# Hybrid retention / attention / mixture-of-experts layer: the low halves of four weight chunks per expert block split between VectorE and GpSimd

## The chip, the cores and the metric

One Trainium2 chip, one NeuronCore. The metric is the device time of one execution in microseconds (us). The engines are called as in the profile: PE (TensorE matmul), PEld (its weight loads), DVE (VectorE), ACT (ScalarE), POOL (GpSimd) and SP (SyncE, which only issues transfers here). A letter q behind an engine means its sequencer.

## The reference, cut to what matters

The layer takes 512 latent tokens and 256 context tokens of width 1024, runs retention and differential attention side by side, merges them, and ends in a mixture of 32 experts with the 4 best experts for each token. Only this last stage is changed:

```
logits = xt @ router_w + router_b;  gate = softmax(top_4(logits))
# token/expert pairs sorted by expert, each expert's group padded to blocks of 128 rows
hh  = xblk @ w1[e] + b1[e]                  # 128x1024 @ 1024x2048
glu = min(hh[:, :1024], 7);  lin = clip(hh[:, 1024:], -7, 7)
act = glu * sigmoid(1.702 * glu) * (lin + 1)
y   = act @ w2[e] + b2[e]                   # 128x1024 @ 1024x1024
out = x_new + g_f * segment_sum(y * gate)
```

All of it is float32. With these inputs there are 33 blocks of 128 rows (32 experts, one of which needs two blocks).

## The kernel before, in words

A float32 product is made of three products of split numbers. ACT rounds a weight chunk to fp32r (the high part, `e_whi`, written by `hi_e`, L1040 and L1041). DVE subtracts it from the chunk as loaded, which gives the low part (`e_wlo`, written by `lo_e`, L1589). PE then multiplies high by high, high by low and low by high (`mm`, L1662).

A weight chunk is 128 partitions x 2048 columns, 1 MB. Each block uses 12 of them: chunks 0 to 7 are w1 (`up`), chunks 8 to 11 are w2 (`down`). Raw chunks lie in 6 slots (`e_raw`), high and low parts in 4 slots each. The loads are issued on SP in the order of the chunks, and a load waits until the low part of the chunk six before it is made (`e_lo`), since that frees its slot. The timeline calls the slots of the parts `whi`, `hhi`, `wlo` and `hlo`; raw chunks are `raw` or `ar`.

Around block i the engines work in this order, all of it written out by hand, each engine in order:

- PE: `up(i)`, which goes chunk by chunk and within a chunk over four groups of 512 columns; then the 8 transposes of the next x (`turn_x`, L2017), `down` of the block before, the 8 transposes of this block's activation (`turn_act`, L2025), and `up(i + 1)`.
- DVE: low part of block i - 1's activation (`act_low`, L1616), low parts of chunks 4 to 10, then `activate`, which begins when `up(i)` has ended: L1600 twice, the low part of chunk 11, L1603, L1606 and L1610 twice each; then the low part of the next x (`x_low`, L1581, twice) and the low parts of chunks 0 to 3 of the next block.
- ACT: the high parts in the same order, the tanh (L1054), the high part of the next x (L1049), then the high parts of chunks 0 to 3 of the next block, and the scaled copy of the output row block, `give_y` (L1067).
- POOL: the bias selector (`next_sel`, L770), the gather of the rows of the block after next (`next_gather`, L777 and L749), the scattered add of a finished block into the result in memory (`scatter`, L786), a wait for that add to land, and the copy of the next list of row numbers (`cur`, L798).

`turn_act` waits for `x_low` (`xt_lo`), since both use the same PSUM banks, and `up(i + 1)` starts when the low part of its chunk 0 is there:

```
    for kk in range(KC):
        pe.wait_ge(e_lo, chunk(i, kk) + 1)
        for b in range(4):
```

Operands of the instructions spoken of below: L1606 and L1610 (`scalar_tensor_tensor`) and L1589 (`tensor_tensor`) read two SBUF tensors; L1600 and L1603 read PSUM; L1581 and L1616 read one PSUM and one SBUF tensor. In the attention stage, POOL squares a 128x512 tile (L722, `tensor_tensor`, two SBUF inputs) and raises 128x8 numbers to a power (L700), while DVE scales and rotates (L1332 to L1351, two SBUF inputs each).

Of the kernel before, what the change touches and what calls it, by code (L numbers as in the profile page):

```python
# [21 lines left out]
F32 = mybir.dt.float32  # L22
# [4 lines left out]
ALU = mybir.AluOpType  # L27
# [3 lines left out]
P = 128  # L31
D = 1024
KC = D // P
L = 512
# [5 lines left out]
COL = 512  # L40
# [3 lines left out]
ERAW = 6  # L44
# [29 lines left out]
OUT0 = GB0 + 4  # L74
MOE0, MOE_N = OUT0 + 4, 12
FIRST = 8


C_ID = 0
# [62 lines left out]
def chunk(i, j):  # L142

    return j if isinstance(i, int) and i == 0 else i * MOE_N - (MOE_N - FIRST) + j

# [11 lines left out]
def raw_slot(i, j):  # L157

    return j % ERAW if isinstance(i, int) and i == 0 else (j - (MOE_N - FIRST)) % ERAW

# [15 lines left out]
def build(nc, a, scratch):  # L176
    mod_d, h2_d, list_d, acc_d, accr_d = scratch
    ctx = ExitStack()
    with ctx:
# [3 lines left out]
        def sem(name):  # L183
            return ctx.enter_context(nc.semaphore(name))
# [63 lines left out]
        e_loaded = [sem(f"e_loaded{k}") for k in range(ERAW)]  # L248
        e_hi = sem("e_hi")
        e_lo = sem("e_lo")  # L250
        e_used = sem("e_used")

        dve_pre = sem("dve_pre")
# [252 lines left out]
        def _(sp):  # L506
# [85 lines left out]
            def load_w1(e, i, j):  # L592

                if isinstance(i, int) and i == 0 and j < NRAW:
                    sp.wait_ge(hi_made, OUT0 - RET0 + j + 1)
                    sp.wait_ge(lo_made, OUT0 - RET0 + j + 1)
                elif not isinstance(i, int) or j >= ERAW:
                    sp.wait_ge(e_lo, chunk(i, j) - ERAW + 1)
                sp.dma_start(e_raw[raw_slot(i, j)], a["exp_w1"][one(e), j * P:(j + 1) * P, :].rearrange(
                    "o p n -> p (o n)")).then_inc(e_loaded[raw_slot(i, j)], 16)  # L600

            def load_w2(e, i, j, k):

                sp.wait_ge(e_lo, chunk(i, j) - ERAW + 1)
                sp.dma_start(e_raw[raw_slot(i, j)].rearrange("p (a n) -> p a n", a=2),
                             a["exp_w2"][one(e), k * 2 * P:(k + 1) * 2 * P, :].rearrange(
                                 "o (a p) n -> p (o a) n", p=P)).then_inc(e_loaded[raw_slot(i, j)], 16)
# [36 lines left out]


            sp.wait_ge(gathered, n_items * 16 + 32)
            sp.wait_ge(y_added, n_items * 16)
            for t in range(LT):
                sp.dma_start(F(A_XG if t == 0 else A_Y if t == 1 else A_GS if t == 2 else A_HT, D),
                             acc_d[t * P:(t + 1) * P, :]).then_inc(acc_back[t], 16)  # L650
# [7 lines left out]
        def _(pool):  # L658
# [32 lines left out]
            def hold():  # L691

                pool.sem_inc(pool_tick, 1)
# [10 lines left out]
            rstd(ss[:, 0:TT], TT, D, st).then_inc(x_rstd, 1)  # L704
            pool.wait_ge(mod_used, 2 * MOD_A + 2)
            pool.wait_ge(pool_pre, ZEROED)
            pool.dma_start(h2_d[L:L + P, :], F(A_ACC, D)).then_inc(s_init, 16)
            pool.dma_start(acc_d[L:L + P, :], F(A_ACC, D)).then_inc(s_init, 16)
            with pool.Fori(0, RET_HEADS) as h:
                pool.wait_ge(o_sq, at(h, LT, LT))  # L710
                rstd(ss[:, 0:LT], LT, DV, Steps(pool, pool_r, h)).then_inc(o_rstd, 1)
# [45 lines left out]
                pool.wait_ge(h2_stored[k], 16 * LT // 2)  # L757
            gather()

            pool.tensor_copy(cur[:, :], listsb[:, 0, :]).then_inc(cur_ready, 1)  # L760
            pool.wait_ge(xt_turned, 2)
            pool.wait_ge(gathered, 16)
            pool.tensor_copy(nxt[:, :], listsb[:, 1, :]).then_inc(pool_m, 1)
# [9 lines left out]
            def next_gather(i, code2):  # L773
# [6 lines left out]
                hold()  # L780
                gather()

            def scatter(i):
                pool.wait_ge(y_out, i * 2 + 2)
                hold()
                pool.indirect_dma_start(acc_d, bass.IndirectOffsetOnAxis(ap=cur[:, 0:1], axis=0),  # L786
                                        F(A_Y, D), None, compute_op=ALU.add).then_inc(y_added, 16)
                pool.wait_ge(y_added, i * 16)
                hold()

            def item(i):
                code = pool.value_load(items_i[0:1, bass.ds(i, 1)], min_val=0, max_val=4 * N_EXPERTS - 1)
                e1 = pool.value_load(items_i[0:1, bass.ds(i + ITEMS + 1, 1)], min_val=0, max_val=N_EXPERTS - 1)
                code2 = pool.value_load(items_i[0:1, bass.ds(i + 2, 1)], min_val=0, max_val=4 * N_EXPERTS - 1)
                next_sel(i, e1)
                next_gather(i, code2)
                scatter(i)
                pool.tensor_copy(cur[:, :], listsb[:, bass.ds(code, 1), :].rearrange(  # L798
                    "p o w -> p (o w)")).then_inc(cur_ready, 1)

            next_sel(0, 1)
            next_gather(0, 2)
            pool.wait_ge(acc_init, 16 * LT)
            with pool.Fori(1, N_EXPERTS) as i:
                item(i)
            with pool.Fori(N_EXPERTS, MAX_BLOCKS) as i:
                with pool.If(i < n_items):
                    item(i)
            scatter(n_items)
            pool.wait_ge(gathered, n_items * 16 + 32)  # L810
            hold()
# [306 lines left out]
        def _(dve):  # L1118
# [105 lines left out]
            lo(RET0, RET_N, 0, 0)  # L1224
            mod_row(11)
            acc = F(A_ACC, KC, L)
            dve.wait_ge(s_init, 16 * (4 + 2))
            dve.wait_ge(h_lo, 2 * KC)
            RS = 7
            with dve.Fori(0, RET_HEADS) as h:  # L1230
# [353 lines left out]
            def lo_e(i, j):  # L1584

                s = raw_slot(i, j)
                dve.wait_ge(e_hi, chunk(i, j) + 1)
                dve.wait_ge(e_loaded[s], rounds(i, j) * 16 + 16)
                V.tensor_tensor(e_wlo[j % ESPL], e_raw[s], e_whi[j % ESPL].bitcast(F32),  # L1589
                                ALU.subtract).then_inc(e_lo, 1)  # L1590

            MS = 4
# [67 lines left out]
        def _(pe):  # L1660
# [368 lines left out]
            def up(i):  # L2029
                pe.wait_ge(sel_ready, i + 1)  # L2030
                for kk in range(KC):
                    pe.wait_ge(e_lo, chunk(i, kk) + 1)
                    for b in range(4):
                        o = ps[:, 2 + b, :]
                        cols = slice(b * COL, (b + 1) * COL)
                        wh, wl = e_whi[kk % ESPL][:, cols], e_wlo[kk % ESPL][:, cols]
                        if kk == 0:
                            last = mm(o, sel[0:96, :], bias[0:96, cols], True, False)
                            if b == 3:
                                last.then_inc(sel_used, 1)  # L2040
                        mm(o, xthi[:, kk, :], wh, False, False)
                        mm(o, xthi[:, kk, :], wl, False, False)
                        last = mm(o, xtlo[:, kk, :], wh, False, kk == KC - 1)
                    last.then_inc(e_used, 1)

            def down(i, at_i, j0):
                pe.wait_ge(act_lo, i * 2 + 2)
                pe.wait_ge(y_out, i * 2 + 2)
                for k in range(MOE_N - FIRST):
                    j = j0 + k  # L2050
                    pe.wait_ge(e_lo, chunk(at_i, j) + 1)
                    for q in range(2):
                        kk = 2 * k + q
                        for c in range(2):
                            o = ps[:, 6 + c, :]
                            cols = slice(q * D + c * COL, q * D + (c + 1) * COL)
                            wh, wl = e_whi[j % ESPL][:, cols], e_wlo[j % ESPL][:, cols]
                            mm(o, acthi[:, kk, :], wh, kk == 0, False)
                            mm(o, acthi[:, kk, :], wl, False, False)
                            last = mm(o, actlo[:, kk, :], wh, False, kk == KC - 1)  # L2060
                    last.then_inc(e_used, 1)
# [112 lines left out]
```

## Time and profile before

| | |
|---|---|
| time, median of 3 | 2650.99 us (2650.47 to 2651.24) |
| the profiled execution | 2651.42 us, span 2649.8 us |
| mean granted clock of TensorE | 0.961 |
| busy: PE, PEld | 2394.2 us (90%), 1842.1 us (70%) |
| busy: DVE, ACT, POOL | 1709.2 us (65%), 1235.8 us (47%), 511.3 us (19%) |
| memory read | 535.65 MB |

The expert stage fills the second half of the span, from about 1380 us to 2630 us. How to read it: the shares are means over all stages; PE is close to full in the expert stage, and the rows below show where it is not. A timeline row gives start, duration, engine, line, what is written and read, the count of merged instructions, and in brackets the idle time before it and what ended it.

### The profile page before, as it was taken

What the parts mean: (1) busy time and instruction counts of PE and PEld (TensorE: products, weight loads), DVE (VectorE), ACT (ScalarE), POOL (GpSimd) and SP (SyncE); (2) the same over time, 40 slices, a digit from 0 to 9 for tenths busy, and PEclk for the clock granted to TensorE, in tenths of its full rate; (3) what the DMA queues carried; (4) which work ended last, traced back from release to release, by engine and by line L of the source; (5) the groups of instructions that cost most, each with busy time, mean ns of one, the idle gap of its engine ahead of it and who ended that gap; (6) DMA issues with size and microseconds to landing.
All of it is one profiled execution on the core that took longest, in us unless ns stands there. A gap on an engine that the chain in (4) does not pass through costs nothing.

```text
span 2649.8 us, 31314 instructions
## 1 busy us (share of the span) xinstructions
PE 2394.2 (90%) x10564; PEld 1842.1 (70%) x10564; DVE 1709.2 (65%) x1667; ACT 1235.8 (47%) x1215; POOL 511.3 (19%) x313
## 2 busy tenths in 40 slices
PE   5999999999998779769878999999999999999994
PEld 1385858677686667657757777777777777777773
DVE  1433324233246635553748999999999999999994
ACT  1221122121122522352236767777677767777672
POOL 2000000000023003100031233333233233322331
PEclk9999999999999889899959999999999999999997
DMA  8811211112131001003347999999999999999994
GB/s 259 301 65 41 70 47 63 63 47 79 43 116 54 11 33 64 32 1 135 135 148 301 375 362 358 370 367 374 362 358 375 370 368 361 364 371 375 361 359 164
DMA packets 145976, 563.29 MB, mean 213 GB/s; under 512 B 17698, under 2 KB 25890, under 8 KB 111842
## 3 DMA queue, kind: packets, MB, share of 16 engines
q1 hardware_dynamic: 127536, 518.05, 51.4%
q0 software_dynamic: 11280, 38.21, 5.4%
q10 hardware_dynamic: 7112, 6.37, 0.8%
q8 instruction: 33, 0.54, 0.1%
q14 instruction: 15, 0.12, 0.0%
HBM read 535.65 MB, written 26.94 MB: 212 GB/s over the span
## 4 chain that ended last, share of the span: by engine, by line
PE 64%; DVE 12%; ACT 10%; issue 9%; DMA 4%; POOL 1%; DVEq 0%; ACTq 0%; POOLq 0%; SPq 0%
PE ps L1662 62%; DVE wlo L1589 3%; ACT whi L1041 3%; ACT ar L957 2%; ACT hhi L1041 2%; DVE nmx L1369 2%; DMA ar<-in_exp_w 2%; DVE yhi L1581 1%; ACT yhi L1049 1%; DVE hlo L1589 1%; DMA cc<-in_c_ctx 1%; ACT ar L1054 1%; DVE ar L1600 1%; PE ps L1831 1%; PE ps L1912 0%
## 5 line engine op out<-in xcount | busy, mean ns | idle before, releaser
L1662 PE MATMUL ps<-whi,yhi 128*128 128x512 f32 x1088 | 382.7, 417 | 0.0
L822 ACT ACTIVATE whi<-raw 128x2048 fp32r<-128x2048 f32 x60 | 115.0, 1917 | 556.0 <-PE ps L1662 554.7
L1589 DVE TENSOR_TENSOR hlo<-raw,hhi 128x2048 fp32r<-128x2048 f32 x132 | 299.5, 2289 | 82.3 <-ACT hhi L1041 82.3
L1662 PE MATMUL ps<-hhi,yhi 128*128 128x512 f32 x1056 | 335.9, 389 | 0.0
L1127 DVE TENSOR_TENSOR wlo<-raw,whi 128x2048 fp32r<-128x2048 f32 x60 | 137.4, 2290 | 307.4 <-ACT whi L822 307.2
L1589 DVE TENSOR_TENSOR wlo<-raw,whi 128x2048 fp32r<-128x2048 f32 x132 | 296.0, 2283 | 0.2 <-DVE ar L1569 0.2
L1041 ACT ACTIVATE whi<-raw 128x2048 fp32r<-128x2048 f32 x132 | 249.4, 1918 | 98.9 <-PE ps L1662 98.9
L1041 ACT ACTIVATE hhi<-raw 128x2048 fp32r<-128x2048 f32 x132 | 252.9, 1916 | 81.2 <-PE ps L1662 81.2
L786 POOL DMA_INDIRECT acc_d<-ar,cur x33 | 209.9, 6361 | 399.0 <-ACT ar L1067 386.1
L1662 PE MATMUL ps<-ar 128*128 128x128 f32 (+4 forms) x1004 | 250.7, 458 | 16.9 <-ACT ar L1027 7.1
L1662 PE MATMUL ps<-whi,hhi 128*128 128x512 f32 x608 | 241.1, 397 | 12.9 <-DVE wlo L1127 6.7
L1662 PE MATMUL ps<-wlo,hhi 128*128 128x512 f32 x608 | 238.8, 393 | 0.0
L1662 PE MATMUL ps<-whi,hlo 128*128 128x512 f32 x608 | 238.6, 392 | 0.0
L1662 PEld LDWEIGHTS ps<-whi,yhi 128*128 128x128 f32 x1088 | 207.6, 191 | 38.4
L1662 PEld LDWEIGHTS ps<-ar 128*128 128x128 f32 (+1 forms) x1004 | 160.0, 214 | 97.3 <-issue 72.3
L1662 PEld LDWEIGHTS ps<-hhi,yhi 128*128 128x128 f32 x1056 | 198.3, 188 | 41.1
L1662 PE MATMUL ps<-wlo,yhi 128*128 128x512 f32 x560 | 219.6, 392 | 0.0
L1662 PE MATMUL ps<-hlo,yhi 128*128 128x512 f32 x528 | 205.4, 389 | 0.0
L1662 PE MATMUL ps<-whi,ylo 128*128 128x512 f32 x560 | 184.9, 397 | 10.9 <-DVE ylo L1616 10.9
L698 POOL TENSOR_SCALAR sm<-ss 128x8 f32<-128x8 f32 (+3 forms) x37 | 14.0, 380 | 902.4 <-ACT ar L897 604.0
L1589 DVE TENSOR_TENSOR wlo<-ar,whi 128x2048 fp32r<-128x2048 f32 x66 | 151.8, 2300 | 29.6 <-ACT whi L1041 29.6
L1662 PE MATMUL ps<-hhi,ylo 128*128 128x512 f32 x528 | 167.9, 389 | 0.0
(245 smaller groups left out, 4245.8 us busy)
## 6 DMA issues: line engine op xcount, KB each, us to landing
raw<-in_exp_w SPq DMA_DIRECT2D x264, 1024.0 KB, 9.2
ar<-in_exp_w SPq DMA_DIRECT2D x132, 1024.0 KB
raw<-in_w_in SPq DMA_DIRECT2D x44, 1024.0 KB, 5.1
raw<-in_w_mod SPq DMA_DIRECT2D x24, 1024.0 KB, 5.3
raw<-in_w_br_ret SPq DMA_DIRECT2D x8, 1024.0 KB, 5.0
ar<-in_x SPq DMA_DIRECT2D x8, 512.0 KB, 10.2
raw<-in_w_br_diff SPq DMA_DIRECT2D x4, 1024.0 KB, 5.1
raw<-in_w_out SPq DMA_DIRECT2D x4, 1024.0 KB, 12.8
```

What stands on the lines that cost most here:

```text
L786: pool.indirect_dma_start(acc_d, bass.IndirectOffsetOnAxis(ap=cur[:, 0:1], axis=0), F(A_Y, D), None, compute_op=ALU.add).then_inc(y_added, 16)
L822: act.activation(whi[:, j % NSPL, :, :], raw[:, s, :, :], ACT.Copy).then_inc(hi_made, 1)
L957: act.activation(F(A_PROB, 2, 2, T)[:, u % 2, s, :], psf[:, (u % 2) * 1536 + s * T:(u % 2) * 1536 + (s + 1) * T], ACT.Exp, bias=nmx[:, u % ...
L1041: act.activation(e_whi[j % ESPL], e_raw[s], ACT.Copy).then_inc(e_hi, 1)
L1049: act.activation(xthi[:, 4 * q:4 * q + 4, :], ps[:, q, :].rearrange("p (c n) -> p c n", c=4), ACT.Copy).then_inc(xt_hi, 1)
L1054: act.activation(F(A_TH, 2, COL)[:, hf, :], F(A_GS, 2, COL)[:, hf, :], ACT.Tanh, scale=0.5 * ALPHA).then_inc(glu_tanh, 1)
L1127: V.tensor_tensor(wlo[:, j % NSPL, :, :], raw[:, s, :, :], whi[:, j % NSPL, :, :].bitcast(F32), ALU.subtract).then_inc(lo_made, 1)
L1369: V.tensor_reduce(nmx[:, u % 2, :], psf[:, s0:s0 + 2 * T].rearrange("p (s n) -> p s n", s=2), AX.X, ALU.max, negate=True).then_inc(mx_done, 1)
L1581: V.tensor_tensor(xtlo[:, 4 * q:4 * q + 4, :], ps[:, q, :].rearrange("p (c n) -> p c n", c=4), xthi[:, 4 * q:4 * q + 4, :].bitcast(F32), A ...
L1589: V.tensor_tensor(e_wlo[j % ESPL], e_raw[s], e_whi[j % ESPL].bitcast(F32), ALU.subtract).then_inc(e_lo, 1)
L1600: V.tensor_scalar(gs[:, hf, :], ps[:, 2 + hf, :], LIMIT, None, ALU.min).then_inc(glu_min, 1)
L1662: return pe.matmul(out, lhsT, rhs, start=start, stop=stop, skip_group_check=skip)
```

## The change

1. `lo_e` on DVE makes only columns 0 to 1023 of the low part of chunks 0 to 3 of every block but the first. POOL makes columns 1024 to 2047 (`low_second`), with its own semaphore `e_low2`.
2. PE waits for `e_low2` before the third group of 512 columns of these chunks in `up`, and before the second half of a chunk in the final `down`. SP waits for both halves before it loads over the raw chunk.
3. On POOL, the order in a block becomes: selector, `settle` (wait for the add issued in the block before, copy `cur`), gather, four `low_second`, then `scatter`, with no wait behind it. Before, it was selector, gather, `scatter`, wait for the add before it, copy `cur`.
4. Two start-up stores signal another semaphore (`y_added` instead of `s_init`), and the waits are moved to fit.

```
+            def settle(i, code):
+                pool.wait_ge(y_added, i * 16 + 16)
+                hold()
+                pool.tensor_copy(cur[:, :], listsb[:, bass.ds(code, 1), :].rearrange(
+                    "p o w -> p (o w)")).then_inc(cur_ready, 1)
+
+            def low_second(i):
+                for j in range(SHARED):
+                    s = raw_slot(i, j)
+                    pool.wait_ge(e_hi, chunk(i, j) + 1)
+                    pool.wait_ge(e_loaded[s], rounds(i, j) * 16 + 16)
+                    hold()
+                    pool.tensor_tensor(out=e_wlo[j % ESPL][:, SPLIT_AT:], in0=e_raw[s][:, SPLIT_AT:],
+                                       in1=e_whi[j % ESPL][:, SPLIT_AT:].bitcast(F32),
+                                       op=ALU.subtract).then_inc(e_low2, 1 if j else MOE_N - SHARED + 1)
+
             def scatter(i):
                 pool.wait_ge(y_out, i * 2 + 2)
+                pool.wait_ge(cur_ready, i)
                 hold()
                 pool.indirect_dma_start(acc_d, bass.IndirectOffsetOnAxis(ap=cur[:, 0:1], axis=0),
                                         F(A_Y, D), None, compute_op=ALU.add).then_inc(y_added, 16)
-                pool.wait_ge(y_added, i * 16)
-                hold()
...
                 next_sel(i, e1)
+                settle(i, code0)
                 next_gather(i, code2)
+                low_second(i + 1)
                 scatter(i)
-                pool.tensor_copy(cur[:, :], listsb[:, bass.ds(code, 1), :].rearrange(
-                    "p o w -> p (o w)")).then_inc(cur_ready, 1)
...
-                V.tensor_tensor(e_wlo[j % ESPL], e_raw[s], e_whi[j % ESPL].bitcast(F32),
+                cols = slice(0, SPLIT_AT if j < SHARED and not (isinstance(i, int) and i == 0) else 2 * D)
+                V.tensor_tensor(e_wlo[j % ESPL][:, cols], e_raw[s][:, cols], e_whi[j % ESPL][:, cols].bitcast(F32),
                                 ALU.subtract).then_inc(e_lo, 1)
...
                     for b in range(4):
+                        if b * COL == SPLIT_AT and kk < SHARED and not (isinstance(i, int) and i == 0):
+                            pe.wait_ge(e_low2, chunk(i, kk) + 1)
...
                         kk = 2 * k + q
+                        if q and j < SHARED:
+                            pe.wait_ge(e_low2, chunk(at_i, j) + 1)
...
-                    sp.wait_ge(e_lo, chunk(i, j) - ERAW + 1)
+                    free = chunk(i, j) - ERAW + 1
+                    sp.wait_ge(e_lo, free)
+                    if not isinstance(i, int) and ERAW <= j < ERAW + SHARED:
+                        sp.wait_ge(e_low2, free)
```

## Rows read from the trace of the kernel before

**Rows 1.** The page, groups of instructions: count, then busy us and mean ns.

```profile
L786 POOL DMA_INDIRECT acc_d<-ar,cur x33 | 209.9, 6361 | 399.0 <-ACT ar L1067 386.1
```

**Rows 2.** Waits, 1430 to 2600 us: total, times, longest.

```profile
PE ps L1662 <- DVE wlo L1589: 32.1, 31, 1.0
```

**Rows 3.** Timeline of DVE around the turn of one block.

```profile
1517.56 1.28 DVE L1603 TENSOR_SCALAR ar<-ps 128x512 f32<-128x512 f32 x2
1518.76 1.28 DVE L1606 SCALAR_TENSOR_TENSOR ar<-ar 128x512 f32<-128x512 f32 x2
1519.96 1.29 DVE L1610 SCALAR_TENSOR_TENSOR ar<-ar 128x512 f32<-128x512 f32 x2
1521.16 1.28 DVE L1581 TENSOR_TENSOR yhi<-ps,yhi 128x512 fp32r<-128x512 f32 x2
1522.36 4.49 DVE L1589 TENSOR_TENSOR wlo<-raw,whi 128x2048 fp32r<-128x2048 f32 x2
1526.76 4.49 DVE L1589 TENSOR_TENSOR hlo<-ar,hhi 128x2048 fp32r<-128x2048 f32 x2
1531.16 1.28 DVE L1616 SCALAR_TENSOR_TENSOR ylo<-ps,ylo 128x512 fp32r<-128x512 f32 x2
```

**Rows 4.** Timeline of ACT, same turn: the high parts of chunks 0 to 3.

```profile
1516.69 3.72 ACT L1041 ACTIVATE whi<-raw 128x2048 fp32r<-128x2048 f32 x2
1520.30 3.90 ACT L1041 ACTIVATE hhi<-ar 128x2048 fp32r<-128x2048 f32 x2
```

**Rows 5.** Timeline of PE, same turn.

```profile
1522.57 1.09 PE L2025 MATMUL ps<-cst,ar 128*128 128x128 f32 x8 [0.33 <-DVE yhi L1581]
...
1524.70 0.39 PE L1662 MATMUL ps<-ar,sel 96*128 96x512 bf16 x1 [1.04 <-DVE wlo L1589]
```

**Rows 6.** Timeline of POOL, same turn: the scattered add.

```profile
1526.17 6.54 POOL L786 DMA_INDIRECT acc_d<-ar,cur  x1 [12.07 <-ACT ar L1067]
```

**Rows 7.** Timeline of POOL in the attention stage.

```profile
1014.00 2.57 POOL L722 TENSOR_TENSOR ar<-ar 128x512 f32<-128x512 f32 x1 [59.48 <-ACT ar L917]
...
1018.11 2.08 POOL L700 TENSOR_TENSOR rs<-sm,half 128x8 f32<-128x8 f32 x1
1020.15 1.04 POOL L722 TENSOR_TENSOR ar<-ar 128x512 f32<-128x512 f32 x1
...
1077.10 1.64 POOL L700 TENSOR_TENSOR rs<-sm,half 128x8 f32<-128x8 f32 x1
```

**Rows 8.** Timeline of DVE in the attention stage, beside rows 7.

```profile
1013.38 2.29 DVE L1127 TENSOR_TENSOR wlo<-raw,whi 128x2048 fp32r<-128x2048 f32 x1 [8.51 <-ACT whi L822]
...
1018.00 0.69 DVE L1338 TENSOR_TENSOR ar<-ar,cst 128x512 f32<-128x512 f32 x1
1018.61 0.90 DVE L1344 TENSOR_TENSOR ar<-ar,cst 128x128 f32<-128x128 f32 x4
...
1020.29 1.45 DVE L1351 TENSOR_TENSOR ar<-ar,rs 128x512 f32<-128x512 f32 x1
```

**Rows 9.** Timeline of POOL at the end: the last two scattered adds.

```profile
2604.30 5.76 POOL L786 DMA_INDIRECT acc_d<-ar,cur  x1 [12.89 <-issue]
...
2627.20 1.57 POOL L786 DMA_INDIRECT acc_d<-ar,cur  x1 [11.80 <-ACT ar L1067]
```

**Rows 10.** Timeline of DVE at the end, beside rows 9.

```profile
2604.11 4.48 DVE L1589 TENSOR_TENSOR hlo<-ar,hhi 128x2048 fp32r<-128x2048 f32 x2
```

**Rows 11.** Windows of 3 us, PE alone: busy (x instructions), granted clock, DMA.

```profile
1407.00:1410.00 3.00, 0.15 (x1) 0.64 0.59 178
1410.00:1413.00 3.00, 2.77 (x11) 0.50 0.00 0
1413.00:1416.00 3.00, 3.00 (x11) 0.72 0.89 314
```

**Rows 12.** Timeline of PE at the turn from block 0 to block 1.

```profile
1409.85 1.97 PE L2025 MATMUL ps<-cst,ar 128*128 128x128 f32 x8 [5.38 <-DVE yhi L1581]
1412.05 0.61 PE L1662 MATMUL ps<-ar,sel 96*128 96x512 bf16 x1 [0.23 <-DVE wlo L1589]
```

More of the change, by code:

```diff
@@ L76 @@
 FIRST = 8
+SHARED = 4
+SPLIT_AT = 1024
 C_ID = 0
@@ L250, in build @@
         e_lo = sem("e_lo")
+        e_low2 = sem("e_low2")
         e_used = sem("e_used")
@@ L602, in load_w2 @@
             def load_w2(e, i, j, k):
-                sp.wait_ge(e_lo, chunk(i, j) - ERAW + 1)
+                free = chunk(i, j) - ERAW + 1
+                sp.wait_ge(e_lo, free)
+                if ERAW <= j < ERAW + SHARED:
+                    sp.wait_ge(e_low2, free)
                 sp.dma_start(e_raw[raw_slot(i, j)].rearrange("p (a n) -> p a n", a=2),
@@ L646, in _ @@
             sp.wait_ge(gathered, n_items * 16 + 32)
-            sp.wait_ge(y_added, n_items * 16)
+            sp.wait_ge(y_added, n_items * 16 + 32)
             for t in range(LT):
@@ L706, in _ @@
             pool.wait_ge(pool_pre, ZEROED)
-            pool.dma_start(h2_d[L:L + P, :], F(A_ACC, D)).then_inc(s_init, 16)
-            pool.dma_start(acc_d[L:L + P, :], F(A_ACC, D)).then_inc(s_init, 16)
+            pool.dma_start(h2_d[L:L + P, :], F(A_ACC, D)).then_inc(y_added, 16)
+            pool.dma_start(acc_d[L:L + P, :], F(A_ACC, D)).then_inc(y_added, 16)
             with pool.Fori(0, RET_HEADS) as h:
@@ L758, in _ @@
             gather()
-            pool.tensor_copy(cur[:, :], listsb[:, 0, :]).then_inc(cur_ready, 1)
             pool.wait_ge(xt_turned, 2)
@@ L787, in scatter @@
                                         F(A_Y, D), None, compute_op=ALU.add).then_inc(y_added, 16)
-                pool.wait_ge(y_added, i * 16)
-                hold()
             def item(i):
-                code = pool.value_load(items_i[0:1, bass.ds(i, 1)], min_val=0, max_val=4 * N_EXPERTS - 1)
+                code0 = pool.value_load(items_i[0:1, bass.ds(i - 1, 1)], min_val=0, max_val=4 * N_EXPERTS - 1)
                 e1 = pool.value_load(items_i[0:1, bass.ds(i + ITEMS + 1, 1)], min_val=0, max_val=N_EXPERTS - 1)
@@ L803, in _ @@
             pool.wait_ge(acc_init, 16 * LT)
+            low_second(1)
             with pool.Fori(1, N_EXPERTS) as i:
@@ L808, in _ @@
                     item(i)
+            end = pool.value_load(count_i[0:1, 1:2], min_val=N_EXPERTS - 1, max_val=MAX_BLOCKS - 1)
+            code_end = pool.value_load(items_i[0:1, bass.ds(end, 1)], min_val=0, max_val=4 * N_EXPERTS - 1)
+            settle(end + 1, code_end)
             scatter(n_items)
@@ L1226, in _ @@
             acc = F(A_ACC, KC, L)
-            dve.wait_ge(s_init, 16 * (4 + 2))
+            dve.wait_ge(s_init, 16 * 4)
+            dve.wait_ge(y_added, 16 * 2)
             dve.wait_ge(h_lo, 2 * KC)
```

## The prediction, as it was made before the changed kernel had run

> **What bounds the kernel now.** I read the page first, for counts [rows 1], then the waits of the expert stage [rows 2], then the timelines of DVE, ACT and PE around the turn from one block to the next [rows 3 to 5]. The waits show that PE, otherwise close to full in this stage, waits once per block for a low part, 1.04 us each time. The timelines show why. When `up` has ended, DVE works through one chain: L1603, L1606 and L1610 from 1517.56, `x_low` (L1581) from 1521.16 to 1522.44, then the low part of chunk 0 from 1522.36 to 1524.65 (4.49 us for two that overlap by 0.09, so 2.29 each). PE has nothing to do for 0.33 us until `x_low` is done, transposes, and waits 1.04 us for chunk 0; `up` begins at 1524.70 [rows 5]. So the end of this DVE chain sets the period of a block. A saving on it shortens every block, and every microsecond put into it lengthens every block. There are 33 blocks [rows 1], hence 33 such turns: 32 before an `up`, one before the final `down`.
>
> Then I looked for what POOL and DVE do to each other, as the change lets both read large SBUF tensors at once. The attention stage shows it. POOL's 128x512 `tensor_tensor` takes 1.04 us; at 1014.00 it took 2.57 and ended at 1016.57, 0.90 after a DVE `tensor_tensor` with two SBUF inputs that ran from 1013.38 to 1015.67 [rows 7, 8]. The other way round, DVE's L1351 started at 1020.29 beside POOL's L722 (1020.15 to 1021.19) and took 1.45 us, where the like instruction L1338 takes 0.69 [rows 7, 8]: it was held 0.76 us and moved only when POOL was about done. So a POOL instruction and a DVE instruction that each read SBUF tensors in this way go one after the other.
>
> **The change part by part.**
>
> *What DVE saves.* The low part of chunk 0 has 1024 columns in place of 2048: half of 2.29, so 1.15 us (the slope of L1338, 512 columns in 0.69, gives 1.2). On the chain that is a gain of 1.14 us per block. The same saving on chunks 1 to 3 comes after `up` has begun and is off the path: PE takes about 2.7 us for a chunk (12 matmuls at some 0.227 us), DVE 2.29 already.
>
> *What POOL adds.* Four `tensor_tensor` of 128x1024 per block. Nearest row: 1.04 us for 512 columns [rows 7], so 2.08 for one and 8.3 for four. 0.90 of the 1.04 came after DVE let go, which leaves about 0.14 of start-up; I take 1.95 us as the time for which one of them holds DVE off. Bounds: 1.7 (if half of the 0.14 to 0.3 of start-up does not double) and 2.1.
>
> *Where they fall.* The first needs the high part of chunk 0, which ACT gives at about 1518.6; the others follow at 1520.4, 1522.3 and 1524.2 [rows 4]. That is in the middle of DVE's chain, and POOL's queue in front of them is empty by then: the gather follows PE's transposes at the end of `up`, and the scatter has been moved behind the four. Now the turn again, instruction by instruction. I let the two engines alternate: whichever waits gets in when the other's instruction ends. Rows for that: POOL's L700 takes 1.64 undisturbed and 2.08 at 1018.11; the extra 0.44 ends where L1338 ends (1018.69), though L1344 was queued right behind [rows 7, 8].
>
> - L1606 first, from 1518.76 to about 1519.4. POOL, chunk 0: 1519.4 to 1521.35.
> - L1606 second to 1521.95. POOL, chunk 1: to 1523.9.
> - L1610 first to 1524.5. POOL, chunk 2: to 1526.45.
> - L1610 second to 1527.05. Then `x_low` to 1528.25; it reads PSUM and one SBUF tensor and can lie beside POOL's chunk 3, 1527.05 to 1529.0.
> - Low half of chunk 0 on DVE: 1529.0 to 1530.15. `up` begins at 1530.2.
>
> Against 1524.70 this is 5.5 us later. As a sum: four POOL instructions of 1.95 = 7.8, less the 1.2 of `x_low` that the last one lies beside, less the 1.14 saved = 5.46. The second halves are then all there before PE asks for them, so `e_low2` costs nothing.
>
> That L1606 and L1610 (`scalar_tensor_tensor`, two SBUF inputs) are held off as `tensor_tensor` is, no row of before shows; it is the step with the most weight. I take it that they are, since they read the same way. If not, see the third rival. The Trainium skill (SBUF — State Buffer, "Who interferes with whom") says that a DVE instruction with two SBUF inputs contends with a GpSimd instruction that reads SBUF, as its second input comes through a shared read interface, and that an instruction with at most one SBUF input, outside its 2-port modes, does not. By that rule the sum stays 5.46; without it for L1606 and L1610, it would be a gain of some 0.5.
>
> The Trainium skill (GPSIMD Engine Reference, "Elementwise — side-by-side cycle accounting") gives 4497 ns for a 128x2048 `tensor_tensor` on GpSimd and 2293 on DVE. The trace agrees with the second (2.29). An estimate from that page is 2.25 us for 1024 columns; with 2.1 in place of 1.95 the sum would be 6.1 per block.
>
> *The clock.* PE is idle from 1522.24 until `x_low` is done at 1528.25: 6.0 us. At the turn from block 0 to block 1 it was idle 5.38 us [rows 12]. There the granted clock was at 0.50, that is 1.2 GHz in place of 2.4, the 8 transposes took 1.97 us in place of 1.09, and the clock was still low when `up` began; the window from 1413 has a mean of 0.72 [rows 11, 12]. 0.72 over 3 us is 1.7 us at the low level, so PE was slow from 1412.05 to 1414.7 and lost half of that, 1.3 us. I expect this at most turns now. The longer transposes (1528.3 to 1530.3) are covered by the wait for chunk 0 except for 0.1. So 1.4 us more per block; bounds 0 (it does not fall) and 2.8 (twice as long).
>
> *The scatter and `cur`.* The wait for the add goes from behind the scatter to before the next gather. The scatter is issued at about 1529 and is held by DVE's run of half low parts until about 1533.6, then takes 1.5. It ends at 1535, 2.5 us later than before (1532.71) in a block longer by more than that. The gather behind `settle` is due only after the next `up`. Cost nothing; the cover is `up`, some 22 us. ACT's `give_y` needs `cur` at 1524, a block later: nothing.
>
> *SP's loads.* A load over chunks 0 to 3 now waits for the later half. In the walk above POOL's halves (to 1529.0) come before DVE's, so the loads keep their place relative to `up`. They have the whole lengthening as extra time to land. Nothing.
>
> *The start-up semaphores* cost nothing: the stores come long before they are asked for.
>
> **The sum.** 5.46 + 1.4 = 6.9 us per turn, times 33 = 227 us. Against the profiled execution (span 2649.8, time 2651.42) that makes 2878 us. The median of the runs is 0.4 us below that execution, which changes nothing. 0.2% (5 us) is about what a measurement can tell from no change.
>
> **The rivals.**
>
> 1. *Only some of POOL's instructions get in front of chunk 0.* If POOL's sequencer needs 0.6 us between them for its waits, the first three hold the port to 1521.35, 1524.5 and 1527.1, the last beside `x_low`, and DVE's chunk 0 is done at 1528.3; the fourth falls behind it. That is +3.6 us per turn, 119 in all, 2770 us; with the clock's 1.4 it is 2816. For it: no row shows POOL instructions that follow each other behind waits of this kind in the expert loop. Against it: L722 began with the end of L700, with a wait and a signal between them [rows 7]. Chance 0.15.
> 2. *DVE keeps the port as long as its instructions follow without a gap, and POOL starves.* For it: the scattered add takes 1.57 us alone, but 6.54 from 1526.17, ending 1.46 after a run of low parts that ended at 1531.25, with boundaries between them at 1526.85 and 1529.0 that it did not use; the add at 2604.30 ended 1.47 after the run that ended at 2608.59 [rows 3, 6, 9, 10]. Then POOL's chunk 0 waits until L1610 is done, `up` starts about 0.3 early, but the half of chunk 3 waits behind chunks 4, 5 and 6 on DVE until DVE has nothing to do, at about 1538.3; it lands at 1540.3, and PE, which wants it at 1535.1, stalls for 5.3 us in the middle of `up`. In all about +5.2 and the clock's 1.4: 33 times 6.6 = 218, 2869 us. Against it: L700 got in at a boundary. Chance 0.12. It gives nearly the forecast's time by another wait (PE on `e_low2` in place of L2025 on `x_low`). If the side that has the port keeps it in both directions, all four of POOL's run in a row without `x_low` beside them: up to 6.7 + 1.4 per turn, 2918 us.
> 3. *L1606 and L1610 are not held off* (the other sign). POOL's first two then run from 1518.95 to 1523.0 beside them, DVE's half of chunk 0 follows at once to 1524.1, and `up` starts 0.5 us earlier; 33 times 0.55 = 18 us, 2633 us. It decides at one point: whether a `scalar_tensor_tensor` beside a POOL instruction stays at 0.68 us. If nothing contended, the gain would be the whole wait of 1.15 per turn, 2613 us; rows 7 and 8 speak against that. Chance 0.09.
> 4. *The change does little*, because the holds just fill the wait it removes. It would take holds of 1.1 us in place of 6.6. Chance 0.03.
>
> **How the numbers follow.** The forecast's case (5.5 with 0 to 2.8 for the clock, hold 1.7 to 2.1) has 0.61 and goes from 2800 to 2940; its likeliest is 2878. Rival 1 has 0.15, rival 2 has 0.12, rival 3 0.09, rival 4 0.03. The range takes in rivals 1 and 2 and leaves out 3, 4 and the outermost of the clock's bounds: 2760 to 2930. Faster by over 0.2%: 0.09; within: 0.03; slower: 0.88.
>
> **What would show it.** POOL's four `tensor_tensor` between L1606 and the low half of chunk 0, each 2 us or more; L1606 and L1610 with a mean far above 0.68; PE's wait before L2025 at about 6 us (before: 0.33) and the granted clock at 0.5 there; blocks of 44 us where they had 37. It is wrong if L1606 and L1610 keep 0.68 us, if PE's wait is on POOL's half inside `up` (rival 2), or if `up` starts less than 4 us late (rival 1).

## The result, and the profile after

The changed kernel takes 2883.38 us (median of 4 runs, 2881.69 to 2885.55), the kernel before 2651.11 us in the same comparison: a ratio of 1.0877, 95% interval 1.0858 to 1.0896, slower. The forecast was 2878 us. The profiled execution has a span of 2882.9 us against 2649.8, 233.1 us more. One of the ten executions of the version with the new order alone (below) took 4317 us, at a mean granted clock of 0.69; it is left out of that version's ratio, and nothing rests on it.

The waits of PE in the expert stage of the changed kernel, 1430 to 2830 us, all that the view lists (total us, times, longest; L2054 is L2025 of before, L1609 is L1581):

```profile
PE ps L2054 <- DVE yhi L1609: 210.9, 31, 7.0
```

PE no longer waits for the low part of chunk 0 [rows 2], and it never waits for POOL's halves. A turn is the stretch from the start of one `up` to the start of the next. PE waits 6.80 us per turn for `x_low`, before the transposes in front of `up`; before, that was 0.33 us [rows 5].

The timeline of DVE in the changed kernel around one turn (L1632 is L1603 of before, L1635 is L1606, L1639 is L1610, L1618 is L1589):

```profile
1712.80 0.68 DVE L1632 TENSOR_SCALAR ar<-ps 128x512 f32<-128x512 f32 x1
1713.40 0.68 DVE L1635 SCALAR_TENSOR_TENSOR ar<-ar 128x512 f32<-128x512 f32 x1
...
1714.00 2.90 DVE L1635 SCALAR_TENSOR_TENSOR ar<-ar 128x512 f32<-128x512 f32 x1
1716.82 2.83 DVE L1639 SCALAR_TENSOR_TENSOR ar<-ar 128x512 f32<-128x512 f32 x1
...
1719.58 2.82 DVE L1639 SCALAR_TENSOR_TENSOR ar<-ar 128x512 f32<-128x512 f32 x1
1722.33 1.27 DVE L1609 TENSOR_TENSOR yhi<-ps,yhi 128x512 fp32r<-128x512 f32 x2
1723.53 2.17 DVE L1618 TENSOR_TENSOR wlo<-raw,whi 128x1024 fp32r<-128x1024 f32 x1
```

And POOL beside it:

```profile
1713.54 2.81 POOL L803 TENSOR_TENSOR wlo<-raw,whi 128x1024 fp32r<-128x1024 f32 x1 [4.81 <-ACT whi L1068]
...
1716.31 2.80 POOL L803 TENSOR_TENSOR wlo<-raw,whi 128x1024 fp32r<-128x1024 f32 x1
...
1719.07 2.79 POOL L803 TENSOR_TENSOR hlo<-ar,hhi 128x1024 fp32r<-128x1024 f32 x1
...
1721.82 2.80 POOL L803 TENSOR_TENSOR hlo<-ar,hhi 128x1024 fp32r<-128x1024 f32 x1
```

Read the two together. The first L1635 takes 0.68 us. POOL's first instruction starts 0.14 us after it and is let in when it ends; the second L1635 then takes 2.90 us, of which 0.68 is its own work. The two engines go on alternating: both L1639 take 2.8 us. `x_low` keeps its 0.68 us per instruction beside POOL's fourth. The half of chunk 0 takes 2.17 us, where a half that is not held takes 1.21. From the start of L1635 to the end of the low part of chunk 0, DVE takes 12.30 us (1713.40 to 1725.70); before it was 5.89 (1518.76 to 1524.65, rows 3). That is 6.41 us more per turn.

The granted clock, in windows of PE alone at the same turn (the third number is PE's busy time, the one behind the bracket the clock):

```profile
1716.00:1719.00 3.00, 0.94 (x5) 1.00 0.48 199
1719.00:1722.00 3.00, 0.00 (x0) 0.79 0.00 0
1722.00:1725.00 3.00, 1.27 (x6) 0.50 0.00 0
1725.00:1728.00 3.00, 2.94 (x11) 0.57 0.33 68
```

and PE's own timeline:

```profile
1723.73 1.96 PE L2054 MATMUL ps<-cst,ar 128*128 128x128 f32 x8 [6.79 <-DVE yhi L1609]
1725.76 0.61 PE L1691 MATMUL ps<-ar,sel 96*128 96x512 bf16 x1
```

While PE is idle the clock falls to 0.50 (1.2 GHz), so the 8 transposes take 1.96 us in place of 1.09 [rows 5], under the cover of DVE's hold. When `up` starts the clock is still low. From the start of `up` to ACT's first high part behind it (chunk 4, which waits for PE's chunk 0) it is 4.81 us, 1725.76 to 1730.57; before it was 4.02, 1524.70 to 1528.72. That is 0.79 us more.

6.41 + 0.79 = 7.20. The first instructions of `up` lie 44.37 us apart in the changed kernel and 37.15 before: 7.22. Over the whole span the 233 us are: 223.5 in the 31 turns between the second `up` and the last, 7.2 behind the start of the last `up`, 0.1 in the turn from block 0 to block 1 (34.29 us against 34.23), and 2.2 before the first `up`. The last term need not be the change's: the first `up` starts at 1376.5 to 1380.0 us in the traces of this case, in no order that follows the versions. In the turn from block 0 to block 1, POOL's first subtraction starts at 1410.82, when both L1639 are done, so in front of `up` it holds nothing but the half of chunk 0.

The scattered add, which now follows POOL's four subtractions, is held for less time than before (6.54 us, rows 6):

```profile
1724.78 2.39 POOL L811 DMA_INDIRECT acc_d<-ar,cur  x1 [0.16 <-issue]
```

### The profile page after: what moved, and what is told of

Same layout as the page of the kernel before. It is cut to its first block, busy times and chain, and to the rows that moved or that the text cites. A ratio compares the mean times of both kernels' runs of the same rounds, so it can differ in the third digit from the quotient of the medians.

```text
span 2882.9 us, 31875 instructions
## 1 busy us (share of the span) xinstructions
PE 2451.3 (85%) x10564; PEld 1881.5 (65%) x10564; DVE 1825.7 (63%) x1667; ACT 1242.2 (43%) x1215; POOL 676.2 (23%) x445
## 4 chain that ended last, share of the span: by engine, by line
PE 60%; DVE 16%; issue 14%; ACT 8%; DMA 2%; DVEq 1%; POOL 1%; ACTq 0%; POOLq 0%; SPq 0%
PE ps L1691 58%; ACT hhi L1068 4%; DVE ar L1639 3%; DVE wlo L1618 3%; ACT ar L984 2%; DVE nmx L1397 2%; DVE ar L1632 1%; DVE yhi L1609 1%; DVE hlo L1618 1%; DVE ar L1629 1%; DVE ar L1635 1%; DMA cc<-in_c_ctx 1%; PE ps L1860 0%; PE ps L1941 0%; DVE ar L1410 0%
## 5 line engine op out<-in xcount | busy, mean ns | idle before, releaser
L1691 PE MATMUL ps<-whi,yhi 128*128 128x512 f32 x1088 | 402.8, 435 | 0.2 <-DVE wlo L1618 0.2
L1618 DVE TENSOR_TENSOR hlo<-raw,hhi 128x2048 fp32r<-128x2048 f32 x132 | 302.5, 2293 | 107.7 <-ACT hhi L1068 107.7
L1154 DVE TENSOR_TENSOR wlo<-raw,whi 128x2048 fp32r<-128x2048 f32 x60 | 137.4, 2290 | 307.8 <-ACT whi L849 307.6
L1618 DVE TENSOR_TENSOR wlo<-raw,whi 128x2048 fp32r<-128x2048 f32 (+1 forms) x132 | 262.5, 2009 | 79.7 <-ACT whi L1068 79.5
L2054 PE MATMUL ps<-cst,ar 128*128 128x128 f32 x264 | 64.8, 427 | 223.1 <-DVE yhi L1609 223.1
L1691 PEld LDWEIGHTS ps<-whi,yhi 128*128 128x128 f32 x1088 | 217.2, 200 | 40.5 <-DVE wlo L1618 0.6
L1691 PE MATMUL ps<-wlo,yhi 128*128 128x512 f32 x560 | 226.8, 405 | 0.0
L803 POOL TENSOR_TENSOR wlo<-raw,whi 128x1024 fp32r<-128x1024 f32 x66 | 183.9, 2805 | 155.4 <-ACT whi L1068 153.4
L2054 PEld LDWEIGHTS ps<-cst,ar 128*128 128x128 f32 x264 | 51.8, 223 | 236.6 <-issue 231.0
```

Of the source, the lines that this page charges most:

```text
L803: pool.tensor_tensor(out=e_wlo[j % ESPL][:, SPLIT_AT:], in0=e_raw[s][:, SPLIT_AT:], in1=e_whi[j % ESPL][:, SPLIT_AT:].bitcast(F32), op=ALU ...
L1154: V.tensor_tensor(wlo[:, j % NSPL, :, :], raw[:, s, :, :], whi[:, j % NSPL, :, :].bitcast(F32), ALU.subtract).then_inc(lo_made, 1)
L1618: V.tensor_tensor(e_wlo[j % ESPL][:, cols], e_raw[s][:, cols], e_whi[j % ESPL][:, cols].bitcast(F32), ALU.subtract).then_inc(e_lo, 1)
L1691: return pe.matmul(out, lhsT, rhs, start=start, stop=stop, skip_group_check=skip)
L2054: last = pe.transpose(ps[:, hf, c * P:(c + 1) * P], F(A_AC, 2, COL)[:, hf, c * P:(c + 1) * P], ident)
```

## The experiments

Each is a version of the changed kernel unless it says otherwise. The runs answer three questions: what part of the change costs it, by which rule POOL and DVE hold each other, and what the clock adds. All ratios are to the kernel before, run on the same chip.

**The new order on POOL, without the sharing.**

```
-SHARED = 4
+SHARED = 0
```

> The changed kernel with SHARED = 0: all low parts are made by DVE again; POOL keeps the new order (settle, gather, scatter with no wait behind it). My theory, that the time is lost where POOL's four reads of SBUF hold DVE's two-input instructions off: no loss here, 2651 us within 8 (the 33 turns keep 37.1 us). Rival, that the later scatter and the moved wait cost it: part or all of the 232 us stays, 2700 us or more.

Measured: 2651.23 us, ratio 0.9999 (0.9989 to 1.0009). The waits of PE are those of before:

```profile
PE ps L1691 <- DVE wlo L1618: 32.1, 31, 1.0
PE ps L2054 <- DVE yhi L1609: 10.2, 32, 0.3
```

The later scatter, the moved wait and `settle` cost nothing, as I expected.

**POOL makes nothing.** `low_second` waits as before and signals, but subtracts nothing. The second halves of the low parts of chunks 0 to 3 are left out.

```
-                    pool.tensor_tensor(out=e_wlo[j % ESPL][:, SPLIT_AT:], ..., op=ALU.subtract).then_inc(
-                        e_low2, 1 if j else MOE_N - SHARED + 1)
+                    pool.sem_inc(e_low2, 1 if j else MOE_N - SHARED + 1)
```

> The changed kernel, in which POOL signals e_low2 but makes no low part: the second halves of the low parts of chunks 0 to 3 are left out (stale numbers are used). Theory: without POOL's reads DVE's chain is 1.08 us shorter than before the change, up starts as soon as PE's transposes are done, and the kernel gains 33 times 1.0 us: 2617 us. If instead the waits and the order of the change cost time by themselves, it stays above 2651 us.

Measured: 2617.34 us, ratio 0.9876 (0.9860 to 0.9893); turns of 36.08 us, 1.07 less than before. PE's whole wait of 1.04 us for chunk 0 is gone; DVE's half of chunk 0 takes 1.21 us in place of 2.29, 1.08 less, where the prediction took 1.14. All waits and signals of the change are in this run, and they cost nothing.

**POOL writes, but does not read.** The same leaving out, with a `memset` of 128x1024 in place of each subtraction.

```
-                    pool.tensor_tensor(out=e_wlo[j % ESPL][:, SPLIT_AT:], ..., op=ALU.subtract).then_inc(
+                    pool.memset(e_wlo[j % ESPL][:, SPLIT_AT:].bitcast(F32), 0.0).then_inc(
```

> The changed kernel, in which POOL writes zeros (memset of 128x1024) in place of its four subtractions: the second halves of the low parts of chunks 0 to 3 are left out. POOL is as busy as with a one-pass instruction, in the same places, but reads nothing from SBUF. If it is POOL's reading that holds DVE's two-input instructions off, L1635 and L1639 stay at 0.68 us and the kernel is as fast as with no POOL work, 2617 us. Rival, that any POOL instruction on SBUF holds them: each hold is then about the memset's own duration, 1 us or so, 3 us per turn, 2750 us.

Measured: 2618.88 us, ratio 0.9887 (0.9870 to 0.9903); turns of 36.08 us. DVE and POOL at one turn of this run, DVE first:

```profile
1694.69 1.28 DVE L1633 SCALAR_TENSOR_TENSOR ar<-ar 128x512 f32<-128x512 f32 x2
1695.89 1.29 DVE L1637 SCALAR_TENSOR_TENSOR ar<-ar 128x512 f32<-128x512 f32 x2
```

```profile
1694.81 0.96 POOL L803 MEMSET wlo<- 128x1024 f32 x1 [4.79 <-ACT whi L1066]
1696.52 0.96 POOL L803 MEMSET wlo<- 128x1024 f32 x1 [0.76 <-ACT whi L1066]
```

POOL is busy in the same place for 0.96 us at a time, and DVE's pairs keep 1.28 us. So it is not that POOL works or writes. What is left is that it reads SBUF. Here POOL reads two tensors at once; an instruction of POOL that reads only one was not run.

**One chunk shared, then two.** For two, the increments of `e_low2` are 9 and 3, so that each wait still means its own chunk.

```
-SHARED = 4
+SHARED = 1        # 2 in the second run
```

> The changed kernel with SHARED = 1: only chunk 0 is shared. Theory of holds: one POOL instruction holds the chain of DVE for 2.2 us, and DVE's chunk 0 is 1.08 us shorter; +1.1 us per turn, 33 times is 37 us, 2688 us, and PE idle for about 2.5 us before L2054, with the clock at full. Rival, that the loss goes with the amount of shared work: a quarter of 232, 2709 us. Rival without holds: 2617 us.

> The changed kernel with chunks 0 and 1 shared. Theory of holds: two POOL instructions in DVE's chain, 4.3 us, less 1.08 saved: 3.3 us per turn, 33 times is 108, 2759 us, and up to 26 us more if the granted clock falls in the gap of 4.7 us. By amount of work it would be half of 232, 2767 us; so it is the step from one to two (72 us by holds, 58 by amount) and the place of PE's wait that tell.

Measured: 2708.57 us with one (1.0217, 1.0200 to 1.0234) and 2814.80 us with two (1.0623, 1.0605 to 1.0640). By the total, the first fits the rival "by amount" (2709) and not mine (2688). The timeline says why. DVE in the first run (the merged last line is the half of chunk 0, 1.21 us, and the whole chunk 1):

```profile
1678.52 3.50 DVE L1635 SCALAR_TENSOR_TENSOR ar<-ar 128x512 f32<-128x512 f32 x2
1681.95 1.28 DVE L1639 SCALAR_TENSOR_TENSOR ar<-ar 128x512 f32<-128x512 f32 x2
1683.15 1.27 DVE L1609 TENSOR_TENSOR yhi<-ps,yhi 128x512 fp32r<-128x512 f32 x2
1684.35 3.41 DVE L1618 TENSOR_TENSOR wlo<-raw,whi 128x1024 fp32r<-128x1024 f32 x2
```

One instruction is held, and the chain from L1635 to chunk 0 is 7.04 us: +1.15, as expected. With two chunks shared it runs from 1696.32 to 1705.53, 9.21 us: +3.32, also as expected. But the turns of the first run come in two lengths: 38.29 us (+1.15, the hold alone) and 39.85, the second in 12 of 30 turns. The long ones are turns with a low clock (windows of PE alone at two turns):

```profile
1683.00:1686.00 3.00, 1.44 (x10) 1.00 0.00 0
1722.00:1725.00 3.00, 2.14 (x12) 0.88 0.09 19
1725.00:1728.00 3.00, 3.00 (x9) 0.55 0.85 317
```

So I had the hold right and the clock wrong: I expected it at full behind a gap of 2.5 us. It fell in about 4 turns of 10, and each time cost 1.56 us.

The run with two misses my range of 2759 to 2785 us by 30 us (the rival "by amount", 2767, misses by more), and again the hold is right and the clock is not. Its turns take 41.7 to 42.8 us, 5.18 more than before on average, of which the hold is 3.32; the other 1.9 us I put down to the clock, from the timeline alone, as no run filled this gap. It was at 0.50 at every turn, from 0.9 to 3.0 us before `up` until 1.2 to 4.4 us into it. The 8 transposes took 1.6 to 2.0 us in place of 1.09, and here nothing covers them: `up` starts as soon as they end. With four chunks shared the hold on chunk 0 covers them, and the clock is back 1.8 us into `up`. So the shorter gap paid more for the clock (1.9 us) than the longer one (0.79).

**PE kept busy in the gap.** Matmuls into a bank that `up` starts afresh; nothing is left out. 9 per block with one chunk shared, 27 with all four.

```
                 down(i - 1, i, FIRST)
+                pe.wait_ge(glu_min, i * 2 + 2)
+                for _ in range(27):        # 9 with SHARED = 1
+                    mm(ps[:, 2, :], acthi[:, 0, :], ylo[:, 0, :], True, True)
                 turn_act(i)
```

> The run with only chunk 0 shared (2708.6 us), with 9 more matmuls per block in PE's gap of 2.5 us. In that run 14 of the turns took 39.85 us and the others 38.29. If the difference is the granted clock, every turn takes 38.29 now, and the time is 2687 us, which is what the hold of one POOL instruction alone gives (33 times 1.15). If not: 2708 us.

> The changed kernel with 27 more matmuls of 128x128 by 128x512 per block in PE's gap between down and turn_act (about 6.1 of its 6.8 us), into a bank that up starts afresh: they add nothing to the result. If the granted clock falls because PE is idle, it stays at 1.00 now; chunk 0 of up takes 4.0 us in place of 4.8, and 31 turns gain 0.8 us each: 2858 us. If the clock had nothing to do with it: 2883 us.

Measured with one chunk: 2689.49 us, ratio 1.0144 (1.0127 to 1.0161); 38.3 us in every turn but the first and the last (without the filling, 12 turns were long, not the 14 of my expectation). More work on PE, and 19 us less than without it (2708.57). The difference between the two lengths of a turn was the clock. With four chunks: 2875.75 us (2864.37 to 2883.08), ratio 1.0831 (1.0806 to 1.0857), 8 us less than the changed kernel where I expected 25; as its runs spread over 19 us, the 8 are barely clear of noise. Its turns are of 43.70 us in 17 of 30 cases and 45.27 in the others. 43.70 is 37.15 + 6.55: the hold by itself, within 0.14 of the 6.41 read from DVE. In the others the clock still fell, just behind the start of `up` (1768.75 at this turn), after 0.77 us and 1.0 us of idle time on either side of the transposes, and that cost 1.57 us:

```profile
1766.00:1769.00 3.00, 1.35 (x10) 1.00 0.00 0
1769.00:1772.00 3.00, 3.00 (x9) 0.50 0.67 188
```

In the changed kernel, behind a far longer gap, all turns are of 44.37. So with four chunks the filling shows the size of the hold, and only partly the clock's share.

**POOL reads 512 columns in place of 1024.**

```
-SPLIT_AT = 1024
+SPLIT_AT = 1536
```

> The changed kernel with SPLIT_AT = 1536: POOL makes 512 columns of each of the four chunks in place of 1024. If a hold is as long as POOL's reading (2.16 us for 1024 columns), it is 1.1 us here; three of them fall in front of x_low and the fourth beside it, and DVE's low part of chunk 0 is 0.57 us shorter than before the change: +2.7 us per turn, 89 us, 2740 us, and with a granted clock that falls in some turns up to 2795. If a hold had a fixed length, or the loss were by the clock alone, it would stay above 2850 us.

Measured: 2769.65 us, ratio 1.0447 (1.0429 to 1.0464); turns of 40.95 us. DVE:

```profile
1726.85 2.38 DVE L1635 SCALAR_TENSOR_TENSOR ar<-ar 128x512 f32<-128x512 f32 x2
1729.15 3.46 DVE L1639 SCALAR_TENSOR_TENSOR ar<-ar 128x512 f32<-128x512 f32 x2
1732.54 1.27 DVE L1609 TENSOR_TENSOR yhi<-ps,yhi 128x512 fp32r<-128x512 f32 x2
1733.74 3.41 DVE L1618 TENSOR_TENSOR wlo<-raw,whi 128x1536 fp32r<-128x1536 f32 x2
```

2.38 in place of 1.28 is one hold of 1.10 us; 3.46 is two of 1.09. Half the columns, half the hold. The last line is two of 1.75 us that overlap by 0.09, so chunk 0 ends at 1735.49; the chain is 8.64 us, +2.75 against an expected 2.7. The rest of the 3.80 per turn is put down to the clock, which is at 0.50 around the start of `up` here too (from 1.1 us before it to 2.3 us into it at this turn); no run took it away with this split.

**The same POOL work behind the start of `up`.** Twice: released by DVE's half of chunk 0, and released by `x_low`.

```
             def low_second(i):
+                pool.wait_ge(e_lo, chunk(i, 0) + 1)       # second run: pool.wait_ge(xt_lo, i * 2 + 2)
                 for j in range(SHARED):
```

> The changed kernel, with POOL's four low parts held back until DVE has made its half of chunk 0 of the same block, so that the same instructions fall behind the start of up. Theory of holds in DVE's chain: up starts 1.0 us earlier than before the change; most of the 232 us goes; what is left are waits of PE for POOL's halves inside up, 1.3 us in chunk 0 and up to 2 in chunks 2 and 3, so 2640 to 2735 us, my value 2690. Rival, that POOL's volume or rate costs the time wherever it lies: 2850 us or more.

> The changed kernel, with POOL's four low parts held back until x_low of the same block is done, so POOL's first request comes about 0.3 us into DVE's low half of chunk 0. If POOL is let in when the DVE instruction in progress ends, its half of chunk 0 is done 3.3 us after x_low, PE waits 0.2 us for it inside up, and the kernel lies at 2620 to 2650 us. If DVE keeps the port through instructions that follow each other, as it did in the run with POOL held back until chunk 0, POOL waits for the fourth low half, is done 6.7 us after x_low, PE waits 3.6 us, and the time is that of that run, 2793 us, within 20.

Measured: 2792.77 us (1.0531, 1.0514 to 1.0549) and 2716.61 us (1.0273, 1.0229 to 1.0318). Both are faster than the changed kernel with the very same instructions, 91 and 167 us less, so place counts and volume does not by itself. Both miss my numbers. In the first, PE's wait is:

```profile
PE ps L1692 <- POOL wlo L804: 107.4, 30, 3.6
```

and POOL, then DVE, at one turn:

```profile
1742.45 7.64 POOL L804 TENSOR_TENSOR wlo<-raw,whi 128x1024 fp32r<-128x1024 f32 x2 [9.77 <-DVE wlo L1619]
```

```profile
1740.95 2.35 DVE L1619 TENSOR_TENSOR wlo<-raw,whi 128x1024 fp32r<-128x1024 f32 x2
1743.22 2.35 DVE L1619 TENSOR_TENSOR hlo<-ar,hhi 128x1024 fp32r<-128x1024 f32 x2
1745.49 1.28 DVE L1646 SCALAR_TENSOR_TENSOR ylo<-ps,ylo 128x512 fp32r<-128x512 f32 x2
```

DVE's four halves run on without a hold until 1745.57, past two ends of instructions at which POOL was waiting. POOL's first gets in after that. This is the starving of the prediction's second rival, which the scattered adds had shown [rows 6, 9, 10]. The clock falls behind this wait too (at 0.50 from 5.2 to 8.6 us into `up` at this turn). In the second run POOL starts at 1720.78, 0.46 us into the first half, and is let in at its end:

```profile
1720.32 4.54 DVE L1619 TENSOR_TENSOR wlo<-raw,whi 128x1024 fp32r<-128x1024 f32 x2
1724.79 6.76 DVE L1619 TENSOR_TENSOR hlo<-ar,hhi 128x1024 fp32r<-128x1024 f32 x2
```

All three later halves on DVE are held. No hold lies in the chain in front of `up`, and the turn is still 39.06 us, 1.9 more than before. I had left out that DVE has no room behind the start of `up` either: held there, it works without a pause through `up` (busy 952 us in 1000, before 915), and PE waits a little for halves in chunk after chunk. `up`, from its start to the transposes behind it, takes 25.4 us in place of 22.8. That is 2.7 more, less the 1.04 saved in front of it, and 0.3 more for `x_low`. Of the 2.7, waits of PE are 1.4; in the other 1.3 PE is busy for longer at the full clock, and no run shows why.

**The clips first, with and without the change.** In `activate`, the two clips that read PSUM go ahead of the low part of chunk 11, where DVE stood idle for 1.91 us.

```
-                between()
                 for hf in range(2):
                     V.tensor_scalar(ac[:, hf, :], ps[:, 4 + hf, :], -LIMIT, LIMIT, ALU.max, ALU.min).then_inc(moe_step, 1)
+                between()
```

> The changed kernel, with the two clips issued ahead of the low part of chunk 11. The same POOL work, DVE's chain from L1635 on 1.2 us earlier. Theory of holds by order of arrival: POOL's first instruction now finds L1639 in front of it, two of the four fall in front of the low half of chunk 0 (one of them partly beside x_low), the other two behind the start of up; up starts about 1 us later than before the change in place of 6.4: 2680 to 2730 us. If the loss is by amount of work or by clock alone, it only gains the 1.2 us per turn: 2843 us.

> The kernel before, nothing shared; in activate the two clips (L1603 of before) are issued ahead of the low part of chunk 11, where DVE waits 1.91 us for ACT. The chain to up gets 1.2 us shorter. If that chain is the bound of a turn, PE's wait for chunk 0 (1.04 us) shrinks to about 0.1 and the kernel gains 33 times 0.9 to 1.1 us: 2618 us. Rival, that the weight loads (DMA 97 per cent busy in the stage) bound it just behind: 2640 us or more.

Measured on the changed kernel: 2708.25 us, ratio 1.0223 (1.0205 to 1.0240). A shift of 1.2 us in DVE's chain gives back 175 us of the 232. Its timeline of DVE:

```profile
1713.50 1.29 DVE L1635 SCALAR_TENSOR_TENSOR ar<-ar 128x512 f32<-128x512 f32 x2
1714.71 3.51 DVE L1639 SCALAR_TENSOR_TENSOR ar<-ar 128x512 f32<-128x512 f32 x2
1718.14 1.28 DVE L1609 TENSOR_TENSOR yhi<-ps,yhi 128x512 fp32r<-128x512 f32 x2
```

POOL's first instruction starts at 1714.85, as the high part of chunk 0 allows, and now finds only the second L1639 to hold. The rest falls beside `x_low` or behind the start of `up`.

Measured on the kernel before: 2615.34 us, ratio 0.9867 (0.9851 to 0.9884). This is faster than both kernels, by 1.3% against the one before. PE's wait for chunk 0 falls from 1.0 to 0.4 us, its wait of 0.33 us for `x_low` is gone, and PE is busy for 990 us of 1000 (before: 964):

```profile
PE ps L1662 <- DVE wlo L1589: 11.1, 30, 0.4
```

The loads did not stop it: they reached 379 GB/s in the same 1000 us, where before had 367.

## Why the prediction was right

- *What bounds a turn* was read rightly: DVE's chain from the end of `up` to the low part of chunk 0. Moving two DVE instructions of that chain (2615 us, 1.20 us per turn) and shortening its last one (2617 us, 1.07 per turn) each gave back most of PE's 0.33 + 1.04 us of waiting.
- *What DVE saves*: taken as 1.14 us, measured 1.08 (2.29 less 1.21).
- *The step with the most weight*, that L1606 and L1610 (two SBUF inputs) are held off by a reading POOL instruction: they took 2.82 to 2.90 us in place of 0.68, and stay at 0.68 when POOL only writes. Here the trace agrees with the rule of the Trainium skill (SBUF — State Buffer, "Who interferes with whom"), in both of its halves: two SBUF inputs against a POOL read are held, against a POOL write they are not. The third rival is out.
- *How long a hold is*: taken as 1.95 us, measured 2.14 to 2.22 (2.90, 2.83 and 2.82 less 0.68). This is the term that was too small; its bounds, 1.7 to 2.1, do not hold the measured value either. Doubling the 1.04 us of the 512-column instruction and taking start-up off once was wrong; halving the columns gave 1.1, so the hold goes by columns, at about 2.1 ns each. Three holds came to 6.5 in place of 5.85, and the fourth cost 0.96 on chunk 0 in place of 0.75. The sum in the chain was 6.41, not 5.46.
- *The order*: they took turns as in the list of the prediction. Rival 1 (a pause between POOL's instructions) is out: the next one starts with the end of the one before. Rival 2 (POOL starves) did not happen in the changed kernel, where PE never waits for POOL's halves; it did in the run that released POOL behind chunk 0. That one version alternates and the other starves seems to hang on the moment at which POOL comes; the prediction had one short instruction (L700) for alternating and the scattered adds against it, so that the right case came was in part luck.
- *The clock*: taken as 1.4 us per turn, measured 0.79 in the changed kernel. Here I took too much: it took the time at the low clock from the turn from block 0 to block 1 (2.65 us into `up`), and here it is 1.8. That the clock falls in the gap was right.
- *The waits on POOL's halves, the scatter, `cur` and the start-up signals* cost nothing, as said: shown by the run with the order alone and by PE's waits. One step to it was wrong: the scatter is not held through the whole run of half low parts; it is let in behind the first half and takes 2.39 us. SP now waits for POOL's halves too (31 times, 3.5 us at most), and none of it came back: in the expert stage ACT waits for no load. No run took this wait away by itself.
- *The number of turns*: taken as 33. The turn from block 0 to block 1 lost 0.1 us, so it is 32; the 2.2 us before the first `up` happen to fill some of the difference.

The two errors of size have opposite signs: 5.46 + 1.4 = 6.86 against 6.41 + 0.79 = 7.20. By the measured terms, 32 times 7.20 is 230 us; the prediction has 33 times 6.86, 226 us. Five microseconds from 2883 is better than the terms were, and that much of it was luck.

## What to carry to other kernels

In these runs, work on POOL that reads SBUF was free only where DVE was not reading two SBUF tensors at the same time, and work that only writes was free; what counts is not how idle POOL is, but what DVE does in the stretch in which POOL's input comes ready. Before sharing an engine's work, look for idle time in its own chain: two independent instructions moved into a wait of 1.9 us gave 1.3% with a change of one line. And a gap on PE has a second price, the clock behind it, which should be added to the first.

## What the runs showed of the hardware that I had not expected

- How little idle time can stand before a fall of the granted clock. In the run with one chunk shared, a gap of 2.54 us with 1.09 us of transposes behind it was followed by a fall in 12 turns of 30. In the run with 27 added matmuls, 0.77 us idle, the transposes and 1.0 us idle were followed by one in 13 of 30. Each time cost 1.56 to 1.57 us. In the kernel before, 0.33 us idle, the transposes and 1.04 us idle were never followed by one. Filling a gap of 2.5 us with 9 matmuls that do nothing made the kernel 19 us faster.
- When POOL and DVE hand over is not settled by these runs. A run of DVE instructions here means instructions with two SBUF inputs that follow each other without a pause. POOL was let in at the end of a DVE instruction when it had come during the first of a run (1713.54, 1720.78, and the scattered add at 1724.78), and starved through the rest of a run when it had come later (1742.45, and the scattered adds at 1526.17 and 2604.30). Two cases do not fit. At 1714.85 POOL came while the first L1639 ran, behind two L1635, and was let in at its end. In the run with one chunk shared, the scattered add came during the second of DVE's low parts (1685.48 to 1687.76) and was let in at its end, though two more followed without a pause:

```profile
1685.98 3.25 POOL L811 DMA_INDIRECT acc_d<-ar,cur  x1 [4.51 <-ACT ar L1094]
```

It ended at 1689.23, 1.47 us behind that instruction, which is about its own time (1.57 us alone, rows 9); its like at 1526.17 also came during the second low part and was passed over at the ends of two of them. So "DVE keeps the port once it has passed it to itself" is not the rule either, and which rule it is stays open.
